# Three convolution inputs of a gated delta layer in the wide product form, and the vectors' transfer behind the sixth piece of weights

## The reference, what is computed

```python
def odd_layer(x, norm_g, w_in, ...):
    proj = rmsnorm(x, norm_g) @ w_in
    xc, zc, qd, kd, vd, zd, a_pre, b_pre = split_cols(proj, OD_SIZES)   # 1024 columns each, a and b 8
    xconv = causal_dwconv(xc, conv_c_w) + conv_c_b                      # four taps along the tokens
    yc = rg_lru(xconv, gate_w, gate_b, lam) * silu(zc)
    qkv = silu(causal_dwconv(concatenate([qd, kd, vd]), conv_d_w))
    q, k, v = split(qkv, 3)                                             # 8 heads of 128
    q, k = l2norm(q), l2norm(k)
    beta, g = sigmoid(b_pre), -exp(a_log) * softplus(a_pre + dt_bias)
    yd = rmsnorm(gated_delta_chunkwise(q, k, v, beta, g), onorm_g) * silu(zd)
    return x + concatenate([yc, yd]) @ w_out
```

## Time and profile before

| what | value |
|---|---|
| runs of the kernel, median | 1914.71 us (1914.64 to 1915.15, 3 runs) |
| the profiled execution | 1914.7 us |
| its span in the trace | 1912.9 us |
| TensorE busy | 1903.1 us |
| VectorE, ScalarE, GpSimd busy | 1217.8, 1015.6, 166.0 us |
| bytes moved | 340.27 MB |

### The profile page before, as it was taken

One profiled execution on the slowest core, in us unless ns is written; L12 is line 12 of the kernel. 1 busy time (PEld: TensorE's weight loads), 2 busy tenths in 40 slices (PEclk: granted clock), 3 DMA queues, 4 the chain that ended last, 5 costly groups with the idle time before them and its releaser, 6 DMA issues.

```text
span 1912.9 us, 26478 instructions
## 1 busy us (share of the span) xinstructions
PE 1903.1 (99%) x10498; PEld 1643.2 (86%) x10498; DVE 1217.8 (64%) x1684; ACT 1015.6 (53%) x1579; POOL 166.0 (9%) x142
## 2 busy tenths in 40 slices
PE   9999999999999999999999999999999999999998
PEld 7888888888899998898888888888888888888886
DVE  6665655555566787687557888645555778754553
ACT  7434445664557765765543335556454344445643
POOL 0000000110002111100001211000000111100110
PEclk9999999999999999999999999999999999999999
DMA  9555545545554444444555554554555555454453
GB/s 351 193 177 187 176 158 186 170 166 182 180 173 160 155 149 160 149 150 160 182 197 189 192 177 167 184 177 156 181 182 187 189 186 176 164 185 171 162 199 132
DMA packets 95034, 340.27 MB, mean 178 GB/s; under 512 B 10704, under 2 KB 11472, under 8 KB 94784
## 3 DMA queue, kind: packets, MB, share of 16 engines
q1 hardware_dynamic: 93392, 333.76, 51.2%
q0 software_dynamic: 944, 3.61, 0.6%
q10 hardware_dynamic: 576, 1.21, 0.2%
HBM read 336.44 MB, written 2.10 MB: 177 GB/s over the span
## 4 chain that ended last, share of the span: by engine, by line
PE 99%; DMA 0%; SPq 0%; ACT 0%; DVE 0%; issue 0%
PE ACC L735 18%; PE ACC L737 18%; PE ACC L736 18%; PE ACC L740 9%; PE ACC L743 9%; PE ACC L742 4%; PE ACC L741 4%; PE ACC L748 3%; PE ACC L749 3%; PE ACC L750 3%; PE PM L851 1%; PE PM L866 1%; PE PM L904 1%; PE PM L888 1%; PE PM L889 1%; PE PM L887 1%
## 5 line engine op out<-in xcount | busy, mean ns | idle before, releaser
L1441 DVE TENSOR_TENSOR WL<-RAW,WH 128x1024 fp32r<-128x1024 f32 (+1 forms) x624 | 794.7, 1289 | 533.1 <-ACT WH L1075 531.6
L1075 ACT ACTIVATE WH<-RAW 128x1024 fp32r<-128x1024 f32 (+1 forms) x626 | 651.0, 1052 | 518.7 <-PE ACC L737 263.4
L735 PE MATMUL ACC<-WH,XHL 128*128 128x512 f32 x1012 | 402.4, 398 | 0.5 <-DVE WL L1441 0.5
L737 PE MATMUL ACC<-WH,XHL 128*128 128x512 f32 x1012 | 394.3, 390 | 0.0
L736 PE MATMUL ACC<-WL,XHL 128*128 128x512 f32 x1012 | 394.0, 389 | 0.0
L740 PE MATMUL ACC<-XHL,WH 128*128 128x512 f32 x704 | 282.3, 401 | 0.0
L743 PE MATMUL ACC<-XHL,WH 128*128 128x512 f32 x704 | 278.4, 396 | 0.0
L737 PEld LDWEIGHTS ACC<-WH,XHL 128*128 128x128 f32 x1012 | 190.0, 188 | 40.2
L735 PEld LDWEIGHTS ACC<-WH,XHL 128*128 128x128 f32 x1012 | 190.1, 188 | 39.2 <-DVE WL L1441 0.9
L736 PEld LDWEIGHTS ACC<-WL,XHL 128*128 128x128 f32 x1012 | 190.2, 188 | 38.5
L742 PE MATMUL ACC<-XHL,WL 128*128 128x256 f32 x704 | 195.9, 278 | 0.0
(11 more groups left out here) (368 smaller groups left out, 2434.4 us busy)
## 6 DMA issues: line engine op xcount, KB each, us to landing
RAW<-in_w SPq DMA_DIRECT2D x621, 512.0 KB, 3.2
X<-in_x SPq DMA_DIRECT2D x4, 512.0 KB, 12.2
RAW<-in_w SPq DMA_DIRECT2D x6, 256.0 KB, 4.2
Y<-in_xT SPq DMA_DIRECT2D x2, 512.0 KB, 11.0
S<-in_bias POOLq DMA_DIRECT2D x8, 128.0 KB, 2.4
S<-in_od_gate_w POOLq DMA_DIRECT2D x1, 1024.0 KB, 5.8
S<-in_final_norm POOLq DMA_DIRECT2D x1, 1024.0 KB, 7.5
out<-Y SPq DMA_DIRECT2D x2, 512.0 KB, 2.6
```

The costliest lines, as they stand in the source:

```text
L735: e.matmul(o, th, hi[:, kk, :], start=f, stop=False)
L737: m = e.matmul(o, tl, hi[:, kk, :], start=False, stop=l)
L1075: e.activation(hi, src, ACT.Copy).then_inc(s_hi)
L1441: e.tensor_tensor(lo, src, hi.bitcast(F32), ALU.subtract).then_inc(s_lo)
```

## The change

The inputs qd0, kd0 and qd1 (the first, second and fourth) take the wide form and are read out as sums. With the first input wide, its first job is called "qds" and ends after four pieces, so that the wait for x's k-tiles (L717) goes to that job, and the turns of x in layer 0's out steps stand one piece behind the jobs' ends instead of two. Layer 1's jobs are then qds0 177 to 180, qds1 181 to 184, kds0 185 to 188, kds1 189 to 192, ab 193, vd0 194 to 201, qds2 202 to 205, qds3 206 to 209; all later ones keep their pieces. So the convolution steps of qd1 stand at 206, 207, 208 for half 0 and at 210, 211, 212 for half 1, where before they were at 210, 211, 212 and 211, 213, 214. The second transfer of VC, columns 16 to 315, is issued by SyncE behind the fifth part of x and the sixth piece of weights, and ACT waits for it at k-tile 8 instead of k-tile 1.

```diff
--- before.py
+++ after.py
@@ -75,7 +75,7 @@
         "conv": (2, 0), "sum": (0, 1), "zc": (0, 2), "add": (0, 2), "rope": (0, 4)}
 BLK = ((0, 0, 0), (128, 1, 0), (256, 1, 1))
 
-SUMMED = (("xc", 0), ("xc", 1))
+SUMMED = (("qd", 0), ("kd", 0), ("qd", 1), ("xc", 0), ("xc", 1))
 
 
 def job_list():
@@ -424,7 +424,7 @@
             put(F(layer, "out", 3) - 0.5, "root")
             if layer < 3:
                 for q in range(8):
-                    put(L(layer, "out", q // 2) + 2, "xt", 8 * (layer + 1) + q, 1)
+                    put(L(layer, "out", q // 2) + (1 if layer == 0 else 2), "xt", 8 * (layer + 1) + q, 1)
                 put(L(layer, "out", 3) + 3, "rms_a", layer + 1)
                 put(L(layer, "out", 3) + 5, "rms_b", layer + 1, 1)
 
@@ -448,7 +448,7 @@
             out_plan(0)
 
         def plan1():
-            b1 = F(1, "qd", 0)
+            b1 = F(1, "qds", 0)
             put(b1 + 18, "decays1", 0, 1)
             put(b1 + 19, "decays2", 0)
             put(b1 + 23, "decays3", 0, 1)
@@ -656,6 +656,7 @@
             load(4)
             load(5)
             load_xT(4)
+            e.dma_start(VC[:, 16:VW], I["vec"][:, 16:VW]).then_inc(s_vec, 16)
             load(6)
             load(7)
             load_xT(5)
@@ -714,7 +715,7 @@
                                 e.wait_ge(s_yl, Y_AT[J.layer, kt // 2])
                     else:
                         xh, xl = XH3[:, kt, :], XL3[:, kt, :]
-                        if j == J_OF[J.layer, {0: "va", 1: "qd"}.get(J.layer, "v0"), 0]:
+                        if j == J_OF[J.layer, {0: "va", 1: "qds"}.get(J.layer, "v0"), 0]:
                             e.wait_ge(s_xl, 16 * J.layer + kt + 1)
                     if w < 128:
                         o, both = acc[0][0:2 * w, 0:256], WH[p % NHL][:, 2 * w * kk:2 * w * kk + 2 * w]
@@ -1055,7 +1056,6 @@
         @block.scalar
         def scalar(e):
             e.dma_start(VC[:, 0:16], I["vec"][:, 0:16]).then_inc(s_vec0, 16)
-            e.dma_start(VC[:, 16:VW], I["vec"][:, 16:VW]).then_inc(s_vec, 16)
 
             def split(p):
                 src, hi, lo = split_parts(p)
@@ -1137,8 +1137,8 @@
                 e.activation(unused, S5[:, 1024:1025], ACT.Copy)
 
             def x0(n):
-                if n < 2:
-                    e.wait_ge((s_vec0, s_vec)[n], 16)
+                if n in (0, 8):
+                    e.wait_ge(s_vec if n else s_vec0, 16)
                 for i, (k, _) in enumerate(X_PARTS):
                     if k == n:
                         e.wait_ge(s_xT[i], 16)
```

## The result

The changed kernel takes 1919.24 us (median of 12 runs, 1918.23 to 1919.48) against 1914.70 of the kernel before (12 runs beside them, 1914.35 to 1915.52). The ratio is 1.0022, with a 95% interval of 1.0015 to 1.0029: slower, by a little more than the 0.2% that the prediction took as the edge of "same".

The account below looks back on a forecast made before the run. TensorE was taken as the bound, its chain of waits 99% of the span. Start -0.4, wide pieces 177 to 192 -1.5 and the stretch from 202 on +5.3 made +3.4: 1918.1 us, range 1911.8 to 1920.2.

Parts of the forecast that it names:

- The start's term: Front of the kernel: moving the vectors' DMA away lets the weights come sooner and saves 0.4 us.
- the third stop: Before TensorE's q step of head 3: it waits 1.6 us for DVE's k step, L1774.
- rival C: At the 3.9 us stop before L958 the clock falls to 1.2 GHz, 1.7 us more: 1919.8; chance 0.12.
- The likeliest case: The forecast itself, whole kernel: 1918.1 us, bounds 1917.1 to 1919.0; chance 0.48.
- Products in wide form: 24 pieces save 0.092 us each, 2.2 us: 1.5 in pieces 177 to 192 and 0.7 in 202 to 209.
- one of the prediction's own signs of being wrong: Start of the kernel: the prediction is wrong if TensorE's stall of 0.5 us remains.
- Turns of x one piece earlier: Layer 0's out: one piece (2.7 us) less of the 3.96 us leaves over 1.2, so 0 cost.
- the evacuation in the first region: Pieces 177 to 192: DVE reductions of 1.22 us replace ACT copies and end each buffer in time, 0 cost.
- The closed chain at 205 to 211: Work put between DVE's and ACT's delta steps adds up: TensorE waits 6.0 us, leaving the stretch 5.3 later.
- ACT and DVE without gaps from piece 205 to 211: Sign expected in the profile after: both engines busy without idle time through these pieces.
- The 1920.6 worked out for a later stop: Under the skill's clock failure mode, the later stop of 1.6 us would cost clock as well, to about 1920.6 us.
- Rival B: Steps at 205 to 211 don't wait, additions go into DVE's and ACT's idle time: -2.6, 1912.1 us; chance 0.22.

Follow-up runs that it names:

- e11_four_wide: As e6_delta_first, with the third input in the wide form too, its other steps at their old pieces: 1912.23 us, ratio 0.9987.
- e5_steps_later: The changed kernel with the fourth input's copies, taps and silu back at their old pieces, reductions and GpSimd's multiplies staying at 205 and 209: 1915.54 us.
- e4_filled_stop: The changed kernel with 24 more products of 256 columns in front of the q step of head 2, where TensorE stands 3.5 us: 1919.08 us.
- e7_all_wide: As e6_delta_first, with all six inputs and xc in the wide form, convolution steps at the feature form's slots: 1918.56 us, ratio 1.002.
- e9_all_wide_norm_later: As e7_all_wide, with the second norm sums five pieces later, at 231 and 232: 1920.02 us, ratio 1.0028.
- e10_all_wide_norm_later_vec_early: As e9_all_wide_norm_later, with the vectors' transfer at the front on ACT's queue as before the change: 1920.25 us, ratio 1.0025.
- e6_delta_first: As e5_steps_later, with the loop over the convolution steps after the delta steps, so delta steps go first at a shared piece: 1913.10 us.

## Why the prediction was right, point by point

The time was forecast as 1918.1 with a range up to 1920.2, and it is 1919.24. The mechanism is the one forecast: DVE's chain through the shared banks makes TensorE wait at 205 to 209, by the sizes worked out. The start's term was wrong, and what stood at the third stop was the slow clock of rival C. The likeliest case's own range, 1917.1 to 1919.0 with the clock at full, was missed by 0.2 us; the measured time is inside the whole range because that reached past C. The chances at the edge were badly divided: 0.70 stood on "same", and the measured median lies 0.7 us beyond that edge, though its interval reaches across it.

- *Products in wide form.* Right: -1.44 for sixteen pieces (forecast -1.5), -0.64 for eight (-0.7), and 0.087 us a piece over 32 pieces in e11_four_wide. The Trainium skill ("TensorE: Matmul & The Clock Gate", Back-to-back issue gap) gives the 2.5 ns a start for an isolated product, and says that in a stream of weight loads and products both set the spacing. The estimate from the 2.5 ns alone, 0.5 us in all, is refuted by all three stretches; the same section's word on streams is the part that fits here.
- *The start.* Wrong, the step "the gain lies between 0 and the 0.5 us of that stall". The stall is 0.4 us in the trace after, so one of the prediction's own signs of being wrong came; and it is missing in ten of the fourteen traces, with the vectors in either place, so it was no measure of what the transfer costs. Nor did I ask who waits next: at piece 16 the read-out by the norm of x lies so close that 0.1 us of a gain could pass. Four pairs of kernels that differ in this alone show no difference (front and later: 1914.72 and 1915.13; 1918.52 and 1918.56; 1920.25 and 1920.02; 1912.39 and 1912.23). In the trace this is 0.57 of the 0.6 us by which the sum was short. The transfer stands behind the fifth part of x and not the fourth, which changes nothing here.
- *Turns of x one piece earlier, the evacuation in the first region.* Right, 0: no wait stands there in any trace.
- *The closed chain at 205 to 211.* Right in place, order and size: L1774 was to end 2.1, 5.3 and 8.2 us late against its old times. Corrected for the 1.3 us by which everything is early (piece 202), it ends 2.0, 5.2 and 8.1 late. The reduction's 1.13 and the taps stretched by 1.0 beside GpSimd's multiply came as worked out. e5_steps_later shows by taking 3.2 us out of the chain that its parts add up: the stop went from 3.52 to 0.35. The sign "ACT and DVE without gaps from piece 205 to 211" was wrong, though: in a circle each engine waits for the next, and ACT stood 6.35 and 4.18 us for DVE's mask, DVE 1.8 to 2.6 us each time for ACT's split.
- *The third stop.* Forecast 1.6, measured 0, and rival C happened with it: the clock fell behind the stop of 3.5 us and cost 1.5, against the 1.7 worked out. The prediction added the two: 3.4 and 1.7 made its 1919.8. e4_filled_stop shows that they are not added: with the clock held up the wait comes back, 1.31 us, and the time is the same. While DVE's chain is the one that is late, what slows TensorE between two waits for it is paid already. That the clock's 1.5 came where 1.6 was forecast is thus no accident, but it was not foreseen. The 1920.6 worked out for a later stop that costs clock as well has nothing for it: behind the stop of 1.31 us the clock stayed at 1.00.
- *Rival B*, that the additions go into idle time of DVE and ACT: refuted by the waits above. Both are idle much of the time there, but their idle time is each one's wait for the other.
- *What was open.* Why the runs' median is 4.5 us over that of before and the profiled pair 4.2 (1918.92 and 1914.7) is not settled. The single executions of the changed kernel lie 1.25 us apart, and the starts of the traces scatter by several tenths.

## What to carry to other kernels

Where two engines hand work to each other in a circle, what is put into the circle adds up, whatever share of their time they are idle; lay the ends of the chain beside the starts of the engine that waits for it, and sum up what the new order puts between. The remedy is to take other work out from between: here the fourth input's steps at their old pieces took +4.5 us to +0.7, doing the handed-over steps first in a shared slot took that to -1.7, and a third input in the wide form to -2.4. And a gain at one wait passes only as far as the next wait's margin, so look that one up before counting it.

## What the runs showed of the hardware

- After 3.5 us without a product the granted clock was still at its full level, and it fell to 1.2 GHz 0.5 us after the products had begun again; it stayed there 3.4 us. After a stop of 3.8 us in e7_all_wide it fell 0.5 us after the restart as well but stayed low for 6.8 us, twice as long. After stops of 4.0 us in e9_all_wide_norm_later and e10_all_wide_norm_later_vec_early it fell 0.2 and 1.1 us before the restart and stayed low for 3.4 and 6.8 us. So neither when it falls nor how long it stays low followed from the length of the stop. A stop filled with products to within 0.64 us kept the clock at 1.00, and so did one of 1.31 us.
- Six multiply-adds of DVE on SBUF took 3.48 us beside one GpSimd multiply of 1.4 us on other data, and 2.45 without it. A single one of the six bore the loss, the first that started inside the multiply; it took 1.52 us in place of 0.47 and ended 0.3 us after it. The 128x128 delta steps of DVE that lay beside such a multiply in e6_delta_first took 0.34 us each, as they do without it.
- A piece of products whose weights change every 256 or 512 columns took 0.08 to 0.09 us less for the same work when they were issued 16 times instead of 24.
